# Mamba-2 scan of a hybrid decoder: one interruption of TensorE per group instead of four, cumulative sums spread by transfers

## Chip, cores and metric

The kernel runs on one core of a Trainium2 chip. The time is the device time of one execution of the whole program in microseconds; it was run three times before, and the median counts. Engines are called TensorE (PE), VectorE (DVE), ScalarE (ACT), GpSimd (POOL) and SyncE (SP).

## What is computed

Two layers over 256 tokens of width 2048, all in float32. A layer projects the normalised input by `w_in`, runs attention and a Mamba-2 mixer side by side, projects both by `w_out`, and adds a SwiGLU block. The part that matters here is the chunked scan, with 16 heads of 64 in 4 groups, a state of 128 and two chunks of 128 tokens:

```python
cum = cumsum(dt * a)                                   # within a chunk, per head
seg = cum_t[..., :, None] - cum_t[..., None, :]
decay = exp(where(causal, seg, -inf))                  # 128 x 128 for each head and chunk
cb = einsum('bclgn,bcsgn->bcgls', cc, bc)              # C times B, per group and chunk
y_diag = einsum('bcgkls,bcsgkp->bclgkp', cb[:, :, :, None] * decay, xdt)
states = einsum('bclgn,bclgk,bclgkp->bcgkpn', bc, decay_to_end, xdt)
y_off = einsum('bclgn,bcgkpn,bclgk->bclgkp', cc, prev, exp(cum))
```

The state of the first chunk is what the second starts from. `y_diag + y_off + d_skip * x` is gated and normalised later.

## The kernel before

**Pairs.** All big products go through one stream of pairs, 368 in a layer, 736 in all. A pair is two weight tiles of 128 x 512 f32 (512 KB in one transfer into `raw`, a ring of four). ScalarE rounds the pair to fp32r (`split`, L866), VectorE makes the remainder (`split_lo`, L1112), and TensorE forms high x high, low x high and high x low: 24 matmuls by 256 columns where weights are stationary (`products_turned`, L697, the first 32 pairs of a layer and the SwiGLU's first half), 12 matmuls by 512 columns elsewhere (`products`, L508). SyncE asks for a pair's tiles when the remainder of the pair four earlier is made.

**Order.** Every engine has its own loop over the layer's pairs `p`, and whatever else it does is written out by hand at a value of `p`. At `p`, ScalarE and VectorE split pair `p + 3` (`LEAD`), and ScalarE waits for TensorE to be done with pair `p - 1` first. So extras of ScalarE at `p` run from TensorE's start of pair `p` on, and those of VectorE a little later. TensorE does its extras of `p` behind the products of pair `p`. Each queue is in order: a wait stops all behind it on that engine.

**The scan.** Pairs 0 to 31 make the channels of the convolution (x, B, C). The step sizes are ready at pair 13; `cumulate` (p = 16) makes the cumulative sums by a matmul with a triangle of ones; `cum_out` (VectorE, p = 17, L1178) copies them to `cums`, negates them into `ncum` and cuts them into three bf16 parts (`cpart`). `turn_cum` (TensorE, p = 19, L593) turns the parts by two bf16 matmuls, and ScalarE copies them to `cumT` (p = 20). The scan goes in 8 units `u`, a group and a chunk each, over pairs 40 to 55:
- even `p`, `scan_a` (L602): four bf16 matmuls with a column of `pick` spread each head's sums over all partitions, one f32 matmul makes C times B. VectorE (`mask_cb`, L1236) adds `ncum` and the causal mask, ScalarE takes the exponential in halves (`decays`, L952), VectorE multiplies by C times B out of PSUM;
- odd `p`, `scan_b` (L620): four f32 matmuls by 64 columns (within the chunk) and one by 256 (the state of chunk 0, or its effect on chunk 1). ScalarE copies the state (L1060); VectorE's `y_out` (L1251) adds up. GpSimd's `scan_inputs` (L445) makes the factors `xdt`, `xde` and `dx`, at most two units ahead.

Around it, `evacuate` (ScalarE, L907) takes the projections q, k, v out of PSUM at p = 39, 47 and 55 with their squares, `qk_sum` (VectorE, L1225) adds the squares at p = 40, 48 and 56, `norm_qk` (GpSimd, L427) scales them, and `turn_qk` (TensorE, L637) turns them, behind pairs 45 and 51 (`KQ_TURNS`) and 59; `scale_qk` (ScalarE, L944) copies them out. From pair 56 on comes attention: `scores` (L649), softmax on VectorE and ScalarE, `turn_p`, `weigh_v` (L669), until pair 74.

Of the kernel before, what the change touches and what calls it, by code (L numbers as in the profile page):

```python
# [19 lines left out]
ALU = mybir.AluOpType  # L20
ACT = mybir.ActivationFunctionType
F32 = mybir.dt.float32
# [4 lines left out]
P = 128  # L27
# [13 lines left out]
def hybrid_decoder(nc, x, attn_norm_w, w_in, q_norm_w, k_norm_w, sinks, conv_w, conv_b, dt_bias, a_log,  # L41
# [40 lines left out]
    KQ_TURNS = [45, 51]  # L82
# [31 lines left out]
    with ctx:  # L114
# [32 lines left out]
        identb = sb("identb", [P, P], BF16)  # L147
        tri = sb("tri", [P, P])
        mask = sb("mask", [P, P])
# [30 lines left out]
        crest = sb("crest", [P, T, HS])  # L180
        PIECE = 32
        cpart = sb("cpart", [P, T, 4, PIECE], BF16)
        pick = sb("pick", [P, HS], BF16)
# [40 lines left out]
        decay = under("decay", [P, 2, HPG, P])  # L224
# [7 lines left out]
        cumT = nc.alloc_sbuf_tensor_at("cumT", [P, TOK], BF16, offset=placed["dtT"])  # L232
# [20 lines left out]
        cpart_ready, cumT_psum, cumT_ready = sem("cpart_ready"), sem("cumT_psum"), sem("cumT_ready")  # L253
# [6 lines left out]
        seg_psum, seg_masked, decay_ready, mt_ready = sem("seg_psum"), sem("seg_masked"), sem("decay_ready"), sem("mt_ready")  # L260
        xdt_ready, y_psum, state_ready, y_ready = sem("xdt_ready"), sem("y_psum"), sem("state_ready"), sem("y_ready")
# [100 lines left out]
        def _(pool):  # L362
# [8 lines left out]
            for s, credit in ((lo_split, RING), (pair_used, RING)):  # L371
# [9 lines left out]
            once(pool.tensor_copy(identb[:, :], ident[:, :]))  # L381
            once(pool.memset(mask[:, :], 0.0))
            once(pool.affine_select(out=mask[:, :], in_=mask[:, :], compare_op=ALU.is_ge, fill=NEG, base=0,
                                    pattern=[[1, P]], channel_multiplier=-1))
# [13 lines left out]
            once(pool.memset(cpart[:, :, :, :], 0.0))  # L398
            once(pool.tensor_tensor(crest[:, 0, :], ident[:, 0:HS], ident[:, PIECE:PIECE + HS], ALU.add))
            once(pool.tensor_tensor(pick[:, :], crest[:, 0, :], ident[:, 2 * PIECE:2 * PIECE + HS], ALU.add))  # L400
# [3 lines left out]
            for layer in range(DEPTH):  # L404
# [40 lines left out]
                def scan_inputs(u):  # L445

                    g, c = u // 2, u % 2
                    b = u % 2
# [8 lines left out]
                    if u == 0:  # L457
# [4 lines left out]
                    if u >= 2:  # L462
                        pool.wait_ge(y_ready, layer * 8 + (u - 1))
                    x_in = heads(ys[:, c, cols])
                    pool.tensor_tensor(heads(xdt[:, b, :]), x_in, spread(dt[:, c, hs]), ALU.mult).then_inc(xdt_ready, 1)
                    if c == 0:
                        pool.tensor_tensor(heads(xde[:, :]), x_in, spread(dte[:, hs]), ALU.mult).then_inc(xdt_ready, 1)
                    pool.tensor_tensor(heads(dx[:, b, :]), x_in, spread(dskip[:, hs]), ALU.mult).then_inc(xdt_ready, 1)

                def gate(z):  # L470
# [3 lines left out]
                    pool.wait_ge(y_ready, layer * 8 + 8)  # L474
# [9 lines left out]
                for u in (0, 1):  # L484
                    scan_inputs(u)
                norm_qk(0)
                for u in (2, 3, 4, 5):
                    scan_inputs(u)
                norm_qk(1)
                for u in (6, 7):  # L490
                    scan_inputs(u)
# [9 lines left out]
        def _(pe):  # L501
# [91 lines left out]
            def turn_cum(layer):  # L593

                pe.wait_ge(cpart_ready, layer + 1)
                for t in range(T):
                    last = nc.tensor.matmul(ps[:, 7, t * P:(t + 1) * P],
                                            cpart[:, t, :, :].rearrange("p a h -> p (a h)"), identb[:, :],
                                            start=True, stop=True)
                last.then_inc(cumT_psum, 1)  # L600

            def scan_a(layer, u):  # L602

                g, c = u // 2, u % 2
                if u == 0:
                    pe.wait_ge(silu_ready, layer * 4 + 4)
                    pe.wait_ge(cum_ready, layer + 1)
                    pe.wait_ge(cumT_ready, layer + 1)
                else:
                    pe.wait_ge(y_ready, layer * 8 + u)  # L610
                    pe.wait_ge(state_ready, layer * 4 + (u + 1) // 2)
                for k in range(HPG):
                    h = g * HPG + k
                    nc.tensor.matmul(ps[:, 6, k * P:(k + 1) * P], pick[:, h:h + 1].broadcast_to([P, P]),
                                     cumT[:, c * P:(c + 1) * P], start=True, stop=True)
                cols = slice(c * P, (c + 1) * P)
                nc.tensor.matmul(ps[:, 7, 0:P], bt[:, g, cols], ctm[:, g, cols], start=True, stop=True) \  # L617
                    .then_inc(seg_psum, 1)

            def scan_b(layer, u):  # L620

                g, c = u // 2, u % 2
                pe.wait_ge(mt_ready, layer * 8 + (u + 1))
# [821 lines left out]
```

## Time and profile before

| | us |
|---|---|
| runs | 2136.22, 2135.30, 2135.31 |
| median | 2135.31 |
| the profiled execution | 2136.34 |
| its span | 2134.6 |
| TensorE busy | 2127.5 |
| VectorE busy | 1235.5 |
| ScalarE busy | 990.9 |
| GpSimd busy | 114.2 |
| DMA, share of 16 engines busy | 61% |

The profile is one execution; its span runs from the first to the last instruction that the profiler saw. TensorE's granted clock is its full one, 2.4 GHz, in every slice of the span. TensorE's records overlap and their ends are modelled, so its pace is read from starts. An f32 matmul shows as two records, an fp32r product and a transpose as one.

### The profile page before, as it was taken

To read this page: it belongs to the slowest core of one execution; us is meant where nothing else is said; L and a number is where in the kernel's file an instruction comes from. 1 tells how busy PE (TensorE), PEld (TensorE's weight loads), DVE (VectorE), ACT (ScalarE), POOL (GpSimd) and SP (SyncE) were. 2 spreads that over 40 slices of the span, in tenths; PEclk is the share of its full clock that TensorE was granted. 3 is DMA by queue.
4 is the path that set the end of the run, shared out by engine and by line. 5 is a ranking of instruction groups with operands and counts; after the bars stand their busy time and mean duration, and the time that the engine had idled before them with its cause. 6 is when DMAs were issued, how large, how long until landed. Compare 5 with 4: busy or idle time off the path is not lost.

```text
span 2134.6 us, 34343 instructions
## 1 busy us (share of the span) xinstructions
PE 2127.5 (100%) x14793; PEld 1952.2 (91%) x14793; DVE 1235.5 (58%) x1464; ACT 990.9 (46%) x1269; POOL 114.2 (5%) x153
## 2 busy tenths in 40 slices
PE   9999999999999999999999999999999999999999
PEld 9988789999999999888899877899999999998887
DVE  5977865555555555544468778555555555554443
ACT  5555754444444444443445557544444444443332
POOL 2023200000000000000000222000000000000000
PEclk9999999999999999999999999999999999999999
DMA  7654456666666666555656544566666666666664
GB/s 221 181 170 133 130 188 189 192 194 196 191 196 193 193 198 192 189 192 193 190 160 188 158 137 132 191 183 196 191 197 194 193 197 191 195 195 201 205 198 138
DMA packets 203287, 392.76 MB, mean 184 GB/s; under 512 B 12240, under 2 KB 12608, under 8 KB 203136
## 3 DMA queue, kind: packets, MB, share of 16 engines
q1 hardware_dynamic: 202752, 390.24, 60.4%
q8 instruction: 116, 1.90, 0.3%
q0 software_dynamic: 352, 0.33, 0.2%
q14 instruction: 35, 0.29, 0.0%
q10 hardware_dynamic: 32, 0.01, 0.0%
HBM read 388.43 MB, written 2.10 MB: 183 GB/s over the span
## 4 chain that ended last, share of the span: by engine, by line
PE 98%; DVE 1%; ACT 1%; DMA 0%; issue 0%; ACTq 0%
PE ps L697 53%; PE ps L508 40%; PE ps L542 2%; PE ps L626 1%; PE ps L677 1%; PE ps L576 0%; PE ps L658 0%; PE ps L657 0%; DMA xr<-in_x_dram 0%; DVE w_lo L1112 0%; PE ps L617 0%; DVE sc L1271 0%; DVE mx L1275 0%; PE ps L533 0%; PE ps L634 0%; PE ps L631 0%
## 5 line engine op out<-in xcount | busy, mean ns | idle before, releaser
L697 PE MATMUL ps<-h_hi,w_hi_s 128*128 128x256 f32 x3320 | 920.7, 277 | 0.0
L697 PE MATMUL ps<-h_hi,w_lo_s 128*128 128x256 f32 x3320 | 918.7, 277 | 0.0
L697 PE MATMUL ps<-h_lo,w_hi_s 128*128 128x256 f32 x3320 | 918.7, 277 | 0.0
L1112 DVE TENSOR_TENSOR w_lo_s<-raw,w_hi_s 128x1024 fp32r<-128x1024 f32 x416 | 510.1, 1228 | 472.5 <-ACT w_hi_s L866 471.8
L866 ACT CAST w_hi_s<-raw 128x1024 fp32r<-128x1024 f32 x416 | 436.1, 1050 | 584.6 <-PE ps L697 559.6
L697 PEld LDWEIGHTS ps<-h_hi,w_hi_s 128*128 128x128 f32 x3320 | 624.7, 188 | 0.2
L697 PEld LDWEIGHTS ps<-h_lo,w_hi_s 128*128 128x128 f32 x3320 | 623.4, 188 | 0.1
L697 PEld LDWEIGHTS ps<-h_hi,w_lo_s 128*128 128x128 f32 x3320 | 623.4, 188 | 0.0
L1112 DVE TENSOR_TENSOR w_lo<-raw,w_hi 128x1024 fp32r<-128x1024 f32 x320 | 397.4, 1246 | 315.1 <-ACT w_hi L866 314.8
L866 ACT CAST w_hi<-raw 128x1024 fp32r<-128x1024 f32 x320 | 335.5, 1049 | 360.5 <-PE ps L508 340.7
L508 PE MATMUL ps<-w_hi,f_hi 128*128 128x512 f32 x956 | 296.3, 391 | 0.0
L508 PE MATMUL ps<-w_lo,f_hi 128*128 128x512 f32 x956 | 294.5, 389 | 0.0
L508 PE MATMUL ps<-w_hi,f_lo 128*128 128x512 f32 x956 | 294.4, 389 | 0.0
L508 PEld LDWEIGHTS ps<-w_lo,f_hi 128*128 128x128 f32 x956 | 179.4, 188 | 37.5
L508 PEld LDWEIGHTS ps<-w_hi,f_lo 128*128 128x128 f32 x956 | 179.4, 188 | 37.5
L508 PEld LDWEIGHTS ps<-w_hi,f_hi 128*128 128x128 f32 x956 | 177.8, 188 | 36.2 <-issue 0.3
L508 PE MATMUL ps<-w_hi,h_hi 128*128 128x512 f32 x320 | 106.1, 413 | 0.0
L508 PE MATMUL ps<-w_hi,h_lo 128*128 128x512 f32 x320 | 99.4, 392 | 0.0
L508 PE MATMUL ps<-w_lo,h_hi 128*128 128x512 f32 x320 | 99.0, 390 | 0.0
L508 PEld LDWEIGHTS ps<-w_hi,h_lo 128*128 128x128 f32 x320 | 60.0, 188 | 13.5
L508 PEld LDWEIGHTS ps<-w_lo,h_hi 128*128 128x128 f32 x320 | 60.1, 188 | 13.4
L508 PEld LDWEIGHTS ps<-w_hi,h_hi 128*128 128x128 f32 x320 | 56.4, 189 | 13.9 <-issue 4.6
(203 smaller groups left out, 989.4 us busy)
## 6 DMA issues: line engine op xcount, KB each, us to landing
raw<-in_w_gate_dram SPq DMA_DIRECT2D x176, 512.0 KB, 3.7
raw<-in_w_up_dram SPq DMA_DIRECT2D x176, 512.0 KB, 3.7
raw<-in_w_down_dram SPq DMA_DIRECT2D x176, 512.0 KB, 4.4
raw<-in_w_in_dram SPq DMA_DIRECT2D x144, 512.0 KB, 3.6
raw<-in_w_out_dram SPq DMA_DIRECT2D x64, 512.0 KB, 4.5
xr<-in_x_dram SPq DMA_DIRECT2D x4, 512.0 KB, 8.4
out_dram<-xr SPq DMA_DIRECT2D x3, 512.0 KB, 6.9
out_dram<-xr SPq DMA_DIRECT2D x2, 256.0 KB, 2.4
```

Source lines behind the costliest of these rows:

```text
L508: done = nc.tensor.matmul(ps[:, bank + t, :], lhs[:, rows + k, t * P:(t + 1) * P], w[:, slot, k, :], start=(first and k == 0 and w is w_hi ...
L542: done = nc.tensor.transpose(ps[0:src.shape[1], bank + at // N, at % N:at % N + src.shape[0]], src, ident[0:src.shape[0], 0:src.shape[0]])
L626: nc.tensor.matmul(ps[:, 7, 2 * P + k * HEAD:2 * P + (k + 1) * HEAD], decay[:, u % 2, k, :], xdt[:, u % 2, k * HEAD:(k + 1) * HEAD], start ...
L677: last = nc.tensor.matmul(ps[half * HEAD:(half + 1) * HEAD, 4, keys * P:TOK], vtok[:, keys, j, :], pT[:, half, keys * TOK:TOK + keys * P], ...
L697: done = nc.tensor.matmul(ps[:, bank + m // 2, m % 2 * TOK:(m % 2 + 1) * TOK], w[:, slot, k, m * P:(m + 1) * P], h[:, rows + k, :], start= ...
L866: nc.scalar.copy(split_buffers(p)[0][:, slot, :, :], raw[:, slot, :, :]).then_inc(hi_split, 1)
L1112: v_.tensor_tensor(lo[:, slot, :, :], raw[:, slot, :, :], hi[:, slot, :, :].bitcast(F32), ALU.subtract).then_inc(lo_split, 1)
```

## The change

`scan_a` and `scan_b` for 8 units go. In their place:
- `turn_cum` turns `cums` itself by two f32 transposes, and ScalarE copies 16 rows into `cum_rows` (p = 20). GpSimd (`spread_cum`) stores them in DRAM, waits, and reads each group's four rows back to all 128 partitions (`cum_all`), a transfer of 512 KB a group; each waits for the one before.
- `c_times_b` makes C times B of all groups and chunks behind pair 39, 8 matmuls in a row into two banks; `keep_cb` (VectorE, p = 40) copies it to SBUF times the triangle `tri`.
- `segments` (VectorE, p = 39, 43, 47, 51) makes the differences of a group, both chunks, by eight instructions, and cuts them at 0 from above; `decays` (ScalarE, p = 40, 44, 48, 52) takes one exponential of 128 x 1024; `times_cb` (VectorE, p = 41, 45, 49, 53) multiplies by C times B.
- `scan` (TensorE, behind pairs 42, 46, 50, 54) does a group's whole scan: the state of chunk 0, eight matmuls within the chunks, and, when ScalarE has copied the state, its effect on chunk 1. `y_out` follows at p = 43, 47, 51, 55.
- `turn_qk` 0 and 1 move from behind pairs 45 and 51 to behind 46 and 54, right after a scan.
- GpSimd's order becomes: spread 0, spread 1, factors of group 0, spread 2, `norm_qk(0)`, spread 3, factors of groups 1 and 2, `norm_qk(1)`, factors of group 3, `norm_qk(2)`. Factors of group g wait for `y_out` of group g - 1.
- `decay` is twice as large; `decay`, `cb` and `cum_all` lie where the mixer's outputs go later. `mask`, `identb`, `cpart`, `crest` and `pick` and what builds them are gone. The buffers of the products stay where they are.

Of the diff, the lines that are taken out stand in the functions above and are left out here, but for the first; new semaphores too.

```diff
@@ -79,7 +79,8 @@
...
     CONV_TURNS = [15, 22, 30]
-    KQ_TURNS = [45, 51]
+    KQ_TURNS = [46, 54]
+    SCAN = [42, 46, 50, 54]
     def weights_stationary(p):
@@ -229,7 +223,13 @@
...
+        cum_rows = nc.alloc_sbuf_tensor_at("cum_rows", [HS, TOK], F32, offset=placed["dtT"])
+        cum_kept = nc.dram_tensor("cum_kept", [DEPTH, HS, TOK], F32, kind="Internal").ap()
+
+
+        cum_all = nc.alloc_sbuf_tensor_at("cum_all", [P, HS, TOK], F32, offset=at_hi)
+        cb = nc.alloc_sbuf_tensor_at("cb", [P, T, GROUPS, P], F32, offset=at_lo)
+        decay = nc.alloc_sbuf_tensor_at("decay", [P, 2, T, HPG, P], F32, offset=at_lo + T * GROUPS * P * 4)
@@ -442,10 +438,20 @@
...
+                def spread_cum(g):
+
+                    hs = slice(g * HPG, (g + 1) * HPG)
+                    if g == 0:
+                        pool.wait_ge(cum_rows_ready, layer + 1)
+                        pool.dma_start(cum_kept[layer, :, :], cum_rows[:, :]).then_inc(cum_stored, 16)
+                        pool.wait_ge(cum_stored, 16 * (layer + 1))
+                    else:
+                        pool.wait_ge(cum_landed[g - 1], 16 * (layer + 1))
+                    pool.dma_start(cum_all[:, hs, :], cum_kept[layer, hs, :].partition_broadcast(P)) \
+                        .then_inc(cum_landed[g], 16)
+
+                def scan_inputs(g):
+
@@ -454,24 +460,25 @@
...
+                    if g == 0:
...
+                    else:
+                        pool.wait_ge(y_ready, layer * 4 + g)
+                    for c in range(T):
+                        x_in = heads(ys[:, c, cols])
+                        if c == 0:
+                            pool.tensor_tensor(heads(xde[:, :]), x_in, spread(dte[:, hs]), ALU.mult).then_inc(xdt_ready, 1)
+                        pool.tensor_tensor(heads(xdt[:, c, :]), x_in, spread(dt[:, c, hs]), ALU.mult).then_inc(xdt_ready, 1)
+                        pool.tensor_tensor(heads(dx[:, c, :]), x_in, spread(dskip[:, hs]), ALU.mult).then_inc(xdt_ready, 1)
...
+                    pool.wait_ge(y_ready, layer * 4 + GROUPS)
@@ -481,14 +488,16 @@
...
+                spread_cum(0)
+                spread_cum(1)
+                scan_inputs(0)
+                spread_cum(2)
...
+                spread_cum(3)
+                scan_inputs(1)
+                scan_inputs(2)
...
+                scan_inputs(3)
@@ -592,47 +601,40 @@
...
+                pe.wait_ge(cum_ready, layer + 1)
+                turned(7, [(t * P, cums[:, t, :]) for t in range(T)], rows_psum)
+
+            def c_times_b(layer):
+
+                pe.wait_ge(silu_ready, layer * 4 + 4)
+                pe.wait_ge(cum_rows_ready, layer + 1)
+                for c in range(T):
+                    cols = slice(c * P, (c + 1) * P)
+                    for g in range(GROUPS):
+                        last = nc.tensor.matmul(ps[:, 6 + c, g * P:(g + 1) * P], bt[:, g, cols], ctm[:, g, cols],
+                                                start=True, stop=True)
+                last.then_inc(cb_psum, 1)
+
+            def scan(layer, g):
+
+                def within(c):
+                    for k in range(HPG):
+                        nc.tensor.matmul(ps[:, 6, c * GW + k * HEAD:c * GW + (k + 1) * HEAD], decay[:, g % 2, c, k, :],
+                                         xdt[:, c, k * HEAD:(k + 1) * HEAD], start=True, stop=True)
+
+                if g == 0:
+                    pe.wait_ge(tok_ready, layer * 3 + 3)
+                    pe.wait_ge(cb_ready, layer + 1)
...
+                    pe.wait_ge(y_ready, layer * 4 + g)
+                pe.wait_ge(xdt_ready, layer * 20 + 5 * (g + 1))
+                pe.wait_ge(mt_ready, layer * 4 + (g + 1))
+                nc.tensor.matmul(ps[:, 7, 0:GW], btok[:, g, :], xde[:, :], start=True, stop=True).then_inc(state_psum, 1)
+                for c in range(T):
+                    within(c)
+                pe.wait_ge(state_ready, layer * 4 + (g + 1))
+                nc.tensor.matmul(ps[:, 7, GW:2 * GW], ctm[:, g, P:2 * P], state[:, :], start=True, stop=True) \
+                    .then_inc(y_psum, 1)
@@ -767,8 +769,10 @@
...
+                        if p == 39:
+                            c_times_b(layer)
+                        if p in SCAN:
+                            scan(layer, SCAN.index(p))
@@ -949,11 +953,10 @@
...
+            def decays(layer, g):
+                act.wait_ge(seg_ready, layer * 4 + (g + 1))
+                d = decay[:, g % 2, :, :, :]
+                nc.scalar.activation(d, d, ACT.Exp).then_inc(decay_ready, 1)
@@ -1041,8 +1044,8 @@
...
+                        act.wait_ge(rows_psum, layer + 1)
+                        nc.scalar.copy(cum_rows[:, :], ps[0:HS, 7, 0:TOK]).then_inc(cum_rows_ready, 1)
@@ -1051,13 +1054,11 @@
...
+                    if p + 2 in SCAN:
+                        decays(layer, SCAN.index(p + 2))
+                    if p in SCAN:
+                        act.wait_ge(state_psum, layer * 4 + (SCAN.index(p) + 1))
+                        nc.scalar.copy(state[:, :], ps[:, 7, 0:GW]).then_inc(state_ready, 1)
@@ -1233,34 +1228,42 @@
...
+            def keep_cb(layer):
+
+                dve.wait_ge(cb_psum, layer + 1)
+                for c in range(T):
+                    ins = v_.tensor_tensor(cb[:, c, :, :], ps[:, 6 + c, :].rearrange("p (g l) -> p g l", g=GROUPS),
+                                           tri[:, :].unsqueeze(1).broadcast_to([P, GROUPS, P]), ALU.mult)
+                ins.then_inc(cb_ready, 1)
+                dve.wait_ge(cb_ready, layer + 1)
+
+            def segments(layer, g):
+
+                dve.wait_ge(cum_landed[g], 16 * (layer + 1))
+                for c in range(T):
+                    for k in range(HPG):
+                        h = g * HPG + k
+                        ins = v_.tensor_scalar(decay[:, g % 2, c, k, :], cum_all[:, h, c * P:(c + 1) * P],
+                                               ncum[:, c, h:h + 1], 0.0, ALU.add, ALU.min)
+                ins.then_inc(seg_ready, 1)
+
+            def times_cb(layer, g):
+                dve.wait_ge(decay_ready, layer * 4 + (g + 1))
+                for c in range(T):
+                    d = decay[:, g % 2, c, :, :]
+                    ins = v_.tensor_tensor(d, d, cb[:, c, g, :].unsqueeze(1).broadcast_to([P, HPG, P]), ALU.mult)
...
+            def y_out(layer, g):
+
+                dve.wait_ge(y_psum, layer * 4 + (g + 1))
+                y, d = ys[:, :, g * GW:(g + 1) * GW], dx[:, 1, :]
+                v_.tensor_tensor(y[:, 0, :], ps[:, 6, 0:GW], dx[:, 0, :], ALU.add)
+                own.done(v_.tensor_tensor(d, ps[:, 6, GW:2 * GW], d, ALU.add))
+                own.done(v_.tensor_tensor(
+                    y[:, 1, :].rearrange("p (h d) -> p h d", d=HEAD), ps[:, 7, GW:2 * GW].rearrange("p (h d) -> p h d", d=HEAD),
+                    ecum[:, g * HPG:(g + 1) * HPG].unsqueeze(2).broadcast_to([P, HPG, HEAD]), ALU.mult))
+                v_.tensor_tensor(y[:, 1, :], y[:, 1, :], d, ALU.add).then_inc(y_ready, 1)
@@ -1386,8 +1387,14 @@
...
+                    if p - 1 in SCAN:
+                        y_out(layer, SCAN.index(p - 1))
+                    if p + 3 in SCAN:
+                        segments(layer, SCAN.index(p + 3))
+                    if p == 40:
+                        keep_cb(layer)
+                    if p + 1 in SCAN:
+                        times_cb(layer, SCAN.index(p + 1))
```

## Rows read from the trace of the kernel before

**Rows 1.** The page: busy time of TensorE, and the chain that ended last
```profile
PE 2127.5 (100%) x14793; PEld 1952.2 (91%) x14793; DVE 1235.5 (58%) x1464; ACT 990.9 (46%) x1269; POOL 114.2 (5%) x153
...
PE 98%; DVE 1%; ACT 1%; DMA 0%; issue 0%; ACTq 0%
```

**Rows 2.** Waits of TensorE, the whole run: us in total, times, longest us
```profile
PE ps L721 <- POOL numbers L377: 2.2, 1, 2.2
...
PE ps L677 <- DVE pT L1284: 0.3, 2, 0.2
```

**Rows 3.** Timeline of TensorE, layer 0: start us, us, engine, line, operation, tiles, count
```profile
128.72 0.62 PE L508 MATMUL ps<-w_hi,h_lo 128*128 128x512 f32 x2
...
133.25 0.61 PE L508 MATMUL ps<-w_lo,h_hi 128*128 128x512 f32 x2
...
141.18 0.40 PE L614 MATMUL ps<-cumT,pick 128*128 128x128 bf16 x4
141.42 0.44 PE L617 MATMUL ps<-ctm,bt 128*128 128x128 f32 x2
141.61 0.71 PE L508 MATMUL ps<-w_hi,h_hi 128*128 128x512 f32 x2
...
144.47 1.00 PE L626 MATMUL ps<-xdt,decay 128*128 128x64 f32 x8
145.30 0.65 PE L634 MATMUL ps<-state,ctm 128*128 128x256 f32 x2
145.60 0.82 PE L508 MATMUL ps<-w_hi,h_hi 128*128 128x512 f32 x2
...
148.56 0.40 PE L614 MATMUL ps<-cumT,pick 128*128 128x128 bf16 x4
```

**Rows 4.** Timeline of TensorE: first spread of the scan and first scores, both layers
```profile
133.71 0.40 PE L614 MATMUL ps<-cumT,pick 128*128 128x128 bf16 x4
...
194.66 0.50 PE L657 MATMUL ps<-kT,qT 64*128 64x128 f32 x4
...
1194.93 0.40 PE L614 MATMUL ps<-cumT,pick 128*128 128x128 bf16 x4
...
1255.89 0.50 PE L657 MATMUL ps<-kT,qT 64*128 64x128 f32 x4
```

**Rows 5.** Timeline of TensorE around the first `turn_qk`, layer 0
```profile
151.85 1.00 PE L626 MATMUL ps<-xdt,decay 128*128 128x64 f32 x8
...
153.17 1.04 PE L542 MATMUL ps<-ident,acc 128*128 128x128 f32 x8
...
156.80 0.40 PE L614 MATMUL ps<-cumT,pick 128*128 128x128 bf16 x4
```

**Rows 6.** Timeline of VectorE, layer 0: a split, masking, `y_out`, square sums
```profile
156.48 1.23 DVE L1112 TENSOR_TENSOR w_lo<-raw,w_hi 128x1024 fp32r<-128x1024 f32 x1 [2.68 <-ACT w_hi L866]
157.62 1.12 DVE L1241 SCALAR_TENSOR_TENSOR decay<-ps,ncum,mask 128x128 f32<-128x128 f32 x4
...
161.61 0.42 DVE L1259 TENSOR_TENSOR dx<-ps,dx 128x256 f32<-128x256 f32 x1 [0.21 <-PE ps L634]
...
162.53 0.42 DVE L1263 TENSOR_TENSOR ys<-ys,dx 128x256 f32<-128x256 f32 x1
...
167.16 1.28 DVE L1232 TENSOR_REDUCE ssq<-ps 128x8 f32<-128x512 f32 x2
```

**Rows 7.** Groups of VectorE by shape: busy us, mean ns of one
```profile
L1215 DVE TENSOR_SCALAR acc<-stage,vecs 128x256 f32<-128x256 f32 x32 | 13.0, 408 | 0.1
```

**Rows 8.** Timeline of VectorE and GpSimd, layer 0: a split beside a product of GpSimd
```profile
147.58 1.63 DVE L1112 TENSOR_TENSOR w_lo<-raw,w_hi 128x1024 fp32r<-128x1024 f32 x1
...
148.09 1.59 POOL L465 TENSOR_TENSOR xdt<-ys,dt 128x256 f32<-128x256 f32 x1
```

**Rows 9.** The page: landing of weight tiles; and the waits of ScalarE on them
```profile
raw<-in_w_in_dram SPq DMA_DIRECT2D x144, 512.0 KB, 3.6
...
ACT w_hi_s L866 <- DMA raw<-in_w_in_dram: 1.3, 2, 1.1
```

More of the change, by code:

```diff
@@ L252, in hybrid_decoder @@
         dtT_ready, dt_turned = sem("dtT_ready"), sem("dt_turned")
-        cpart_ready, cumT_psum, cumT_ready = sem("cpart_ready"), sem("cumT_psum"), sem("cumT_ready")
+        rows_psum, cum_rows_ready = sem("rows_psum"), sem("cum_rows_ready")
+        cum_stored, cum_landed = sem("cum_stored"), [sem(f"cum_landed{g}") for g in range(4)]
         dt_abs, dt_exp, dta_ready = sem("dt_abs"), sem("dt_exp"), sem("dta_ready")
@@ L593, in turn_cum @@
             def turn_cum(layer):
[L595 to L608, printed above, removed]
-                else:
[L610 to L618, printed above, removed]
@@ L620, in scan_b @@
-            def scan_b(layer, u):
-                g, c = u // 2, u % 2
-                pe.wait_ge(mt_ready, layer * 8 + (u + 1))
-                pe.wait_ge(xdt_ready, layer * 20 + (5 * g + 3 + 2 * c))
-                for k in range(HPG):
-                    nc.tensor.matmul(ps[:, 7, 2 * P + k * HEAD:2 * P + (k + 1) * HEAD], decay[:, u % 2, k, :],
-                                     xdt[:, u % 2, k * HEAD:(k + 1) * HEAD], start=True, stop=True)
-                if c == 0:
-                    if g == 0:
-                        pe.wait_ge(tok_ready, layer * 3 + 3)
-                    last = nc.tensor.matmul(ps[:, 6, 0:GW], btok[:, g, :], xde[:, :], start=True, stop=True)
-                else:
-                    pe.wait_ge(state_ready, layer * 4 + (g + 1))
-                    last = nc.tensor.matmul(ps[:, 6, 0:GW], ctm[:, g, P:2 * P], state[:, :], start=True, stop=True)
-                last.then_inc(y_psum, 1)
+                pe.wait_ge(cum_ready, layer + 1)
@@ L651, in scores @@
                 if a == 0:
-                    pe.wait_ge(y_ready, layer * 8 + 8)
+                    pe.wait_ge(y_ready, layer * 4 + GROUPS)
                 else:
@@ L769, in _ @@
                             conv_out(layer, CONV_TURNS.index(p))
-                        if 40 <= p < 56:
-                            (scan_a, scan_b)[p % 2](layer, (p - 40) // 2)
+                        if p == 39:
+                            c_times_b(layer)
+                        if p in SCAN:
+                            scan(layer, SCAN.index(p))
                         if p in KQ_TURNS:
@@ L950, in scale_qk @@
                 last.then_inc(qkT_ready, 1)
-            def decays(layer, u):
-                for half in range(2):
-                    act.wait_ge(seg_masked, layer * 16 + (2 * u + half + 1))
-                    d = decay[:, u % 2, 2 * half:2 * half + 2, :]
-                    nc.scalar.activation(d, d, ACT.Exp).then_inc(decay_ready, 1)
+            def decays(layer, g):
+                act.wait_ge(seg_ready, layer * 4 + (g + 1))
+                d = decay[:, g % 2, :, :, :]
+                nc.scalar.activation(d, d, ACT.Exp).then_inc(decay_ready, 1)
             def exps(layer, a):
@@ L1043, in _ @@
                     if p == 20:
-                        act.wait_ge(cumT_psum, layer + 1)
-                        nc.scalar.copy(cumT[:, :], ps[:, 7, 0:TOK]).then_inc(cumT_ready, 1)
+                        act.wait_ge(rows_psum, layer + 1)
+                        nc.scalar.copy(cum_rows[:, :], ps[0:HS, 7, 0:TOK]).then_inc(cum_rows_ready, 1)
                     if p == 19:
@@ L1053, in _ @@
                         to_tokens(layer, CONV_TURNS.index(p))
-                    if 40 <= p < 56:
-                        u = (p - 40) // 2
-                        if p % 2 == 0:
-                            decays(layer, u)
-                        elif u % 2 == 0:
-                            act.wait_ge(y_psum, layer * 8 + (u + 1))
-                            nc.scalar.copy(state[:, :], ps[:, 6, 0:GW]).then_inc(state_ready, 1)
+                    if p + 2 in SCAN:
[3 more added lines that the diff above has]
+                        nc.scalar.copy(state[:, :], ps[:, 7, 0:GW]).then_inc(state_ready, 1)
                     if p in KQ_TURNS:
@@ L1388, in _ @@
                         cum_out(layer)
-                    if 40 < p < 56:
-                        (mask_cb, y_out)[p % 2](layer, (p - 40) // 2)
+                    if p - 1 in SCAN:
[6 more added lines that the diff above has]
+                        times_cb(layer, SCAN.index(p + 1))
                     if p in (40, 48, 56):
```

72 lines of the change are left out of this document (4 added, 68 removed).

## Prediction

> **What bounds the kernel now.** I read the page first: TensorE is busy for 2127.5 us of the span of 2134.6, and the chain that ended last runs over TensorE for 98% of it [rows 1]. Then I asked what TensorE waited for: its longest wait in the whole run is 2.2 us at the start, and all its waits on other engines come to some 3 us [rows 2]. So the time is the length of TensorE's own instruction stream, and a change pays by what it takes out of that stream and costs what it makes TensorE wait. The span is 1.7 us short of its execution's 2136.34 us, and that is 1.03 us above the median of 2135.31; I take differences within the execution and set them on the median. About 0.2% (4.3 us) is what a measurement here can tell from no change.
>
> **The price of an interruption.** I read TensorE's timeline by starts, because the ends overlap. Undisturbed, 20 products take from 128.72 to 133.25, so a pair of 12 takes 2.72 us [rows 3]. `scan_a` and the next pair take from 141.18 to 144.47, 3.29 us, so this interruption costs 0.57. Of it the four bf16 spreads (`pick`) take 0.24, C times B 0.19 to the next start; 0.21 is what its two passes are worth at the pace below, and about 0.12 is left, which shows as slower first products behind it. `scan_b` and its pair take from 144.47 to 148.56, 4.09 us, so 1.37: the four matmuls by 64 columns run as 8 records in 0.83 (0.104 each), the one by 256 columns is worth twice two passes, 0.43, and again some 0.12 is left [rows 3]. I call 0.12 the price of breaking the products. Each f32 matmul is two records, and a pass by 64 columns costs the same 0.10 as one by 128, so the weight load sets it.
>
> **The stretch before.** From the first insertion behind pair 40 to the first scores behind pair 56 it is 194.66 - 133.71 = 60.95 us in layer 0, and 1255.89 - 1194.93 = 60.96 in layer 1 [rows 4]. Sixteen pairs are 43.49; 17.46 us is the scan with two `turn_qk` (4.95 against 4.09 us for the interval with it, 0.86 each [rows 5]).
>
> **The stretch after, if TensorE never waits.** One C times B block: 8 matmuls, 16 passes at 0.104 = 1.66, with the break 1.78. Four scans, each 0.43 (state) + 16 passes at 0.104 = 1.66 (within) + 0.43 (off) + 0.12 = 2.64: 10.56. Two `turn_qk`, still glued to a scan: 1.72. Sum 14.06, against 17.46: 3.40 less. As a check from the other side: 32 bf16 spreads at 0.06 are 1.92 and 11 breaks fewer (16 to 5) at 0.12 are 1.32, 3.24 in all; the rest is what the first unit lost. `turn_cum` exchanges two bf16 matmuls at 0.06 for two f32 transposes at 0.10 (8 in about 0.8 [rows 5]): +0.1. So -3.3 us in a layer, -6.6 in both.
>
> **What may become late.** I walk the in-order queues of ScalarE and VectorE against TensorE. An f32 product of two tensors by 1024 columns repeats every 1.14 us [rows 6] and needs 1.22 alone, so VectorE makes about one column in 1.04 ns, and an instruction behind another costs about 0.07 more. `segments` is eight tensor_scalars by 128 columns; the trace has none of this shape. The nearest row is the same operation, SBUF to SBUF with pointer scalars, 408 ns at 256 columns [rows 7]: 0.27 alone at 128 and about 0.20 in a row, 1.6 for eight. The upper bound is the old masking, four in 1.12 [rows 6], 0.28 each, 2.2 for eight; the lower bound is two columns at a time, 0.13 each, 1.0 for eight. I take 1.6. `times_cb` and `keep_cb` are two by 512 columns, as the reduce that takes 1.28 [rows 6]: 1.25. `y_out` for both chunks is two gaps of 0.46 and two of 0.34 [rows 6]: 1.60.
> The tightest place is the scan of group 2 behind pair 50, since evacuation, square sums, `turn_qk` 0 and group 2's factors meet there. Count from TensorE's end of pair 46. Scan 1 lasts to 2.52; `turn_qk` and the break to 3.50; pair 50 ends at 3.50 + 4 x 2.72 = 14.37. VectorE's split of pair 50 starts 3.31 behind the start of `turn_qk`, as now from 153.17 to 156.48 [rows 5, 6], at 5.83. From there it has no gap: split 1.14, `y_out` 1.60, `segments` 1.60 (10.17), split of 51, 1.14 + 0.4 because GpSimd's `scan_inputs(2)` runs then (a split beside GpSimd took 1.63 and GpSimd 1.59 [rows 8]) (11.71), square sums 1.20, split of 52, 1.14, `times_cb` 1.25: 15.30, and TensorE sees it at 15.36. It waits 1.0 us. At the two bounds of `segments`, with and without the crowding, this is 0.0 to 1.6, and to 2.4 if two more instructions are crowded. The same walk leaves 0.6 us of slack at group 0 (Exp's table is loaded first, C times B's product stands ahead), 1.7 at groups 1 and 3, and 0.3 at the first scores, where `y_out` of group 3 comes late and two pairs without a break between make TensorE sooner; I put 0.1 there. Where a split is late it has 4 us or more before its pair is used. The state copy takes 0.6 us with its hand-over and hides under 1.66 us of within-chunk matmuls. What GpSimd does for a group waits only for the previous `y_out` and is ready 3 us before its scan, `norm_qk` and the last broadcast ahead of it included; this cover would go if the group's five products took 6 us instead of 3 to 4.
> The transfers: per layer one store of 16 KB and four broadcasts of 512 KB, each as large as a weight tile, which lands in 3.6 us [rows 9]. Three are issued between pairs 21 and 30 and the last near pair 43, each needed 10 us or more later. A weight tile is asked for when the split four pairs earlier ends and is cast at the start of its fourth pair ahead: 5 us of slack behind its 3.6, and 5 more before TensorE needs it. ScalarE's largest visible wait on weight tiles is 1.3 us in all [rows 9]. I cost them at nothing. The constants dropped at the start (mask, bf16 identity, picks) were built by GpSimd under the first pairs: nothing. The buffers of the products keep their places, so their pace stays.
> **Sum:** -3.3 + 1.0 + 0.1 = -2.2 us in a layer, -4.4 in all: 2131.9 against the profiled 2136.34, or 2130.9 against the median.
>
> **A rule of the skill against the row.** The row says that VectorE's tensor_scalar on f32 makes one column at a time (408 ns for 256; at two it would need about 0.28). The Trainium skill, VectorE: DVE Perf Modes, section "Mode 2×_2P — use both read ports for one tensor", says that an f32 tensor_scalar between SBUF operands gets two. By that rule `segments` would be as its lower bound; by the row it is 1.6, and I go by the row.
>
> **Rivals.**
> - No wait worth the name. `segments` at its lower bound ends 0.6 us sooner and without crowding another 0.4: the wait is about 0, and the whole 6.6 us arrive less 0.2: 2128.9. This is the outcome that the skill's rule above gives. Against it speak the tensor_scalar row and the crowded split. Chance 0.22.
> - VectorE becomes the bound in the stretch: `segments` at 0.28 each, three crowded instructions, and the delay carries into the scores. Each layer waits 2.0 to 3.0 us: 2132.7 to 2134.7, 2133.5 as its middle. For it: VectorE has 9 us of work without a gap there. Chance 0.17.
> - A break has no price of its own: the 0.12 belongs to the f32 passes themselves. Then only the spreads go, 1.92 + 0.2 - 0.1 = 2.0 in a layer, less the wait of 1.1: -1.8 in all, 2133.5. Against it: slow first products behind each of the 16 insertions. Chance 0.04.
> - Slower: the broadcasts hold up weight tiles between pairs 21 and 33. All eight read a few rows for 128 partitions, and no row shows such a transfer. It decides from the point where one of them delays a tile by over 10 us. If each takes three times a weight tile, 10.8 us, and blocks the tiles behind it, TensorE loses 0.8 at each, 6.4 in all: 2130.9 + 6.4 = 2137.3. The Trainium skill, DMA: Bandwidth & Descriptors, section "SWDGE vs HWDGE vs iDMA", says that an engine takes turns between the queues of GpSimd and of the others, which speaks against blocking; no row here shows both kinds at once under load. Chance 0.07.
>
> **How the numbers follow.** The forecast has 0.50. A wait under 1.06 us a layer puts it past 0.2% (2131.0), a larger one leaves it within: 0.27 and 0.23. Faster: 0.27 + 0.22 = 0.49. Same: 0.23 + 0.17 + 0.04 = 0.44. Slower 0.07. The range takes in no wait with 0.35 us more saved in a layer, 2128.0, and waits of 3 us a layer, 2134.8.
>
> **What would show it.** Between the first insertion behind pair 39 and the first scores, TensorE's timeline should take 17 x 2.72 + 14.06 = 60.3 us and about 1.1 of waits; scans at 2.64 each; a wait of TensorE on VectorE's product with C times B of about 1 us, once a layer, at the third scan; `segments` at 0.27 us alone; broadcasts of 4 to 6 us that nobody waits for. The forecast is wrong if TensorE waits elsewhere, above all in the products or at the scores, if the third scan does not wait, or if breaks saved do not shorten the stream.

## The result, and the profile after

The changed kernel takes 2142.53 us (median of six, 2142.34 to 2145.16) against 2135.49 for the one before beside it: a ratio of 1.0035, with a 95% interval of 1.0025 to 1.0044. It is slower, by 7.0 us, where 4.4 us less were forecast, and it lies outside the range of 2128.0 to 2134.8 us. The profiled execution took 2142.81 us, 6.5 more than the profiled one before.

The page of the changed kernel, as [rows 1], and its waits of TensorE (us in total, times, longest), as [rows 2]:

```profile
PE 2126.7 (99%) x14729; PEld 1954.1 (91%) x14729; DVE 1236.8 (58%) x1444; ACT 988.0 (46%) x1245; POOL 118.9 (6%) x157
...
PE 96%; DVE 2%; ACT 1%; issue 1%; DMA 0%; ACTq 0%
```

```profile
PE ps L632 <- DVE decay L1254: 4.9, 2, 2.4
PE ps L551 <- DVE mx L1283: 2.6, 2, 1.3
...
```

Two waits are new, each once a layer: the scan of group 2 waits 2.4 us for the product with C times B, and the third `turn_qk`, behind pair 59, waits 1.3 us for VectorE's second score. In the kernel before, the timelines of TensorE and of VectorE have this `turn_qk` and the end of the score it needs as

```profile
205.65 1.07 PE L542 MATMUL ps<-ident,stage 128*128 128x128 f32 x8
```

```profile
205.35 0.15 DVE L1280 TENSOR_TENSOR mx<-sink,mx 128x4 f32<-128x4 f32 x1
```

The score ended at 205.50, so the margin was 0.15 us.

ScalarE's evacuation of q, which stands at the head of the work that leads to this score, starts at the end of pair 55, here in the kernel before and in the changed one:

```profile
190.67 1.27 ACT L918 ACTIVATE stage<-ps,rs 128x512 f32<-128x512 f32 x2 [0.26 <-PE ps L508]
```

```profile
193.27 1.27 ACT L922 ACTIVATE stage<-ps,rs 128x512 f32<-128x512 f32 x2 [0.56 <-PE ps L517]
```

The first scores start at 194.66 [rows 4] and at 195.88 (below), so the evacuation was 3.99 us ahead of them and is now 2.61 ahead: behind pair 55 no `scan_b` stands any more that held TensorE back. Of these 1.38 us the margin covers 0.15, and 1.23 are left of the 1.28 that were measured.

TensorE's timeline, layer 0, with the extras of the scan (start us, us, engine, line, tiles, count; as [rows 3, 4]):

```profile
130.95 1.95 PE L614 MATMUL ps<-ctm,bt 128*128 128x128 f32 x16
...
140.91 0.59 PE L632 MATMUL ps<-xde,btok 128*128 128x256 f32 x2
141.34 1.89 PE L622 MATMUL ps<-xdt,decay 128*128 128x64 f32 x16
143.07 0.65 PE L636 MATMUL ps<-state,ctm 128*128 128x256 f32 x2
...
171.52 0.67 PE L632 MATMUL ps<-xde,btok 128*128 128x256 f32 x2 [2.43 <-DVE decay L1254]
...
195.88 0.50 PE L659 MATMUL ps<-kT,qT 64*128 64x128 f32 x4
```

From C times B to the first scores it is 195.88 - 130.95 = 64.93 us, and 66.56 in layer 1. In the kernel before the same stretch, from the end of pair 39, took 60.95 + 2.72 = 63.67 [rows 4, 3]. Both layers make the same moves, yet the second is 1.6 us longer. TensorE's timeline behind the wait in layer 1, and a table of stretches (columns: us, busy us and count of PE, PEld, DVE, ACT and POOL, granted clock, DMA share, GB/s), show why:

```profile
1235.10 1.02 PE L632 MATMUL ps<-xde,btok 128*128 128x256 f32 x2 [2.44 <-DVE decay L1254]
1235.91 3.52 PE L622 MATMUL ps<-xdt,decay 128*128 128x64 f32 x16
1239.22 1.17 PE L636 MATMUL ps<-state,ctm 128*128 128x256 f32 x2
```

```profile
160.00:170.00 10.00, 9.09 (x41) 7.18 (x39) 9.49 (x17) 6.71 (x9) 3.78 (x6) 1.00 0.27 75
170.00:174.00 4.00, 2.48 (x19) 2.46 (x20) 2.93 (x5) 1.32 (x2) 3.84 (x3) 0.97 0.78 216
174.00:178.00 4.00, 4.00 (x12) 3.16 (x12) 3.77 (x6) 0.00 (x0) 3.92 (x3) 0.61 0.78 252
...
1234.00:1236.00 2.00, 0.90 (x3) 0.76 (x4) 2.00 (x3) 0.00 (x0) 2.00 (x1) 0.82 0.65 179
1236.00:1242.00 6.00, 6.00 (x24) 5.43 (x23) 2.82 (x6) 1.31 (x2) 5.34 (x5) 0.50 0.75 227
1242.00:1244.00 2.00, 2.00 (x10) 1.67 (x9) 2.00 (x6) 0.00 (x0) 1.82 (x4) 0.97 0.00 0
```

Behind the wait of layer 1 the granted clock is 0.50, which is 1.2 GHz instead of 2.4, and the sixteen passes take 3.52 us instead of 1.89. In layer 0 the clock stays full for some 2 us more and falls for a shorter time. By the clock column, 4 x 0.03 + 4 x 0.39 = 1.7 us are lost in layer 0 and 2 x 0.18 + 6 x 0.50 + 2 x 0.03 = 3.4 in layer 1. The third `turn_qk`'s wait of 1.28 us has no such thing behind it.

Now VectorE and GpSimd before the wait, layer 0; the first line is `segments` for group 0, for comparison:

```profile
130.71 1.65 DVE L1246 TENSOR_SCALAR decay<-cum_all,ncum 128x128 f32<-128x128 f32 x8
...
162.82 0.42 DVE L1266 TENSOR_TENSOR ys<-ys,dx 128x256 f32<-128x256 f32 x1
163.17 3.54 DVE L1246 TENSOR_SCALAR decay<-cum_all,ncum 128x128 f32<-128x128 f32 x8
166.62 1.22 DVE L1113 TENSOR_TENSOR w_lo<-raw,w_hi 128x1024 fp32r<-128x1024 f32 x1
167.76 1.28 DVE L1227 TENSOR_REDUCE ssq<-ps 128x8 f32<-128x512 f32 x2
168.96 1.22 DVE L1113 TENSOR_TENSOR w_lo<-raw,w_hi 128x1024 fp32r<-128x1024 f32 x1
170.09 1.29 DVE L1254 TENSOR_TENSOR decay<-decay,cb 128x512 f32<-128x512 f32 x2
```

```profile
163.33 0.61 POOL L473 TENSOR_TENSOR xde<-ys,dte 128x256 f32<-128x256 f32 x1 [14.64 <-DVE ys L1266]
163.90 0.61 POOL L474 TENSOR_TENSOR xdt<-ys,dt 128x256 f32<-128x256 f32 x1
...
165.62 0.61 POOL L475 TENSOR_TENSOR dx<-ys,dskip 128x256 f32<-128x256 f32 x1
```

The end of `y_out` releases both `segments` (by VectorE's queue) and GpSimd's factors (by its semaphore), so they run side by side. The eight instructions, 1.65 us for group 0 where GpSimd is still, take 3.54. GpSimd's five products keep their step of 0.57 us.

### The profile page after: what moved, and what is told of

Same layout as the page of the kernel before. It is cut to its first block, busy times and chain, and to the rows that moved or that the text cites. A ratio compares the mean times of both kernels' runs of the same rounds, so it can differ in the third digit from the quotient of the medians.

```text
span 2141.1 us, 34156 instructions
## 1 busy us (share of the span) xinstructions
PE 2126.7 (99%) x14729; PEld 1954.1 (91%) x14729; DVE 1236.8 (58%) x1444; ACT 988.0 (46%) x1245; POOL 118.9 (6%) x157
## 4 chain that ended last, share of the span: by engine, by line
PE 96%; DVE 2%; ACT 1%; issue 1%; DMA 0%; ACTq 0%
PE ps L699 53%; PE ps L517 38%; PE ps L551 2%; PE ps L622 1%; DVE w_lo L1113 1%; PE ps L679 1%; DVE mx L1278 0%; DVE sc L1274 0%; PE ps L585 0%; DVE decay L1246 0%; ACT sc L966 0%; ACT w_hi L870 0%; DVE ssq L1227 0%; PE ps L636 0%; DMA xr<-in_x_dram 0%
```

## Experiments

Each stands beside runs of the kernel before on its chip, whose median was 2135.4 to 2135.9 us. In each case theory and rival are as on record before the run.

**1. Fill the wait.** Ten idle products of ident with itself go to TensorE ahead of the wait at scan 2; nothing else changes.

```diff
+                if g == 2:
+                    pe.wait_ge(qkT_ready, layer * 3 + 1)
+                    for _ in range(10):
+                        nc.tensor.matmul(ps[:, 5, 0:P], ident[:, :], ident[:, :], start=True, stop=True)
```

> TensorE makes ten idle f32 matmuls (about 2.1 us) where it waited 2.43 us for group 2's factors in each layer. Theory (the wait makes the clock fall, and the fall costs 5.2 us in both layers): the wait shrinks to 0.2 to 0.4 us, the granted clock stays 1.00 everywhere, about 2137.3 us, 5 less than the changed kernel. Rival (the clock falls because of the long run of f32 passes, whatever came before): the fall stays, 2142.5 or more.

Measured: 2139.58 us (2137.59 to 2140.65), ratio 1.0017 [1.0007, 1.0026], the profiled execution 2137.59, with the mean clock at 1.000 in all ten. The scan still starts as late as before (0.2 us of its wait are left), the fill only takes the place of the wait, and 5.2 us of the profiled time are gone. By the clock column the fall had cost 5.1 us, so the two agree, and the waits alone do not explain the result. But 5.2 is one execution, the fastest of ten. By the medians the gain is only 3.0 us: six of the ten times lie 2 to 3 us above the profiled one, with the clock at full, and what they hold stays open. The rival, a fall that comes whatever stood ahead of the passes, is out.

**2. GpSimd's factors behind the segments.** The factors of groups 1 to 3 wait for `seg_ready` too.

```diff
                         pool.wait_ge(y_ready, layer * 4 + g)
+                        pool.wait_ge(seg_ready, layer * 4 + g + 1)
```

> GpSimd starts the factors of groups 1 to 3 only when the group's segments are made. Theory (the segments took 3.54 us instead of 1.65 because GpSimd's five products ran beside them): segments 1.65 us in every group, wait before scan 2 about 0.9 us instead of 2.43, no fall of the clock, 2134 to 2135. Rival (segments are slow for another reason, as the place or the landing of the spread sums): 3.5 us again, 2142.5.

Measured: 2136.85 us (2135.38 to 2140.87), ratio 1.0009 [0.9999, 1.0019]. The durations of the eight segments of group 2 (ns, least, median, most) and the timeline of VectorE behind them:

```profile
L1247 DVE TENSOR_SCALAR decay<-cum_all,ncum x8: 277/279/280, 162.9 to 164.3; 128x128 f32<-128x128 f32 x8
```

```profile
166.81 1.58 DVE L1114 TENSOR_TENSOR w_lo<-raw,w_hi 128x1024 fp32r<-128x1024 f32 x1
168.31 2.12 DVE L1255 TENSOR_TENSOR decay<-decay,cb 128x512 f32<-128x512 f32 x2
```

In the changed kernel the same eight were 276/649/660. So what slowed them was GpSimd, and nothing in themselves; the rival is out. But the wait went only from 2.4 to 1.8 us, not to the expected 0.9: the factors now run beside a split (1.58 instead of 1.22) and the product with C times B (2.12 instead of 1.29), 1.2 us of the 1.9 won. Crowding was moved more than removed. In eight of ten executions the mean clock stayed full, in two it was lower (2140.87 and 2140.78 us). Only the profiled execution, one of the eight, has a trace; if the wait was 1.8 us in the two as well, a wait of this length lowers the clock sometimes.

**3. Segments one pair earlier.** They then run where GpSimd has nothing to do for group 2.

```diff
-                    if p + 3 in SCAN:
-                        segments(layer, SCAN.index(p + 3))
+                    if p + 4 in SCAN:
+                        segments(layer, SCAN.index(p + 4))
```

> Segments are made one pair earlier, out of the rush behind pair 47 and away from GpSimd's factors. Theory: segments 1.65 us, wait before scan 2 at most 0.3 us, clock 1.00, and the waits of 1.28 us before the last turn_qk stay: 2142.5 - 10 = 2132 to 2133. If even this waits over 1 us there, the evacuation and the square sums set it. Rival (merging gains nothing on TensorE, breaks have no price): 2136 to 2138 without any wait at scan 2.

Measured: 2133.84 us (2132.81 to 2134.79), ratio 0.9993 [0.9984, 1.0002], clock full in all ten. The waits of TensorE:

```profile
PE ps L551 <- DVE mx L1283: 2.6, 2, 1.3
PE ps L723 <- POOL numbers L380: 2.2, 1, 2.2
PE ps L632 <- DVE decay L1254: 1.2, 2, 0.6
```

`segments` for group 2 takes 1.64 us. The wait at scan 2 is 0.6 us, where at most 0.3 were expected. This one step, moved by a pair, takes 8.7 us off the changed kernel: 3.7 of wait and the whole fall of the clock. The `turn_qk` wait is untouched, so it is a matter of its own.

**4. Each broadcast twice.** The second lands in a buffer that nobody reads; the chain of transfers still goes one after the other.

```diff
+                    pool.dma_start(cum_again[:, :, :], cum_kept[layer, hs, :].partition_broadcast(P)) \
+                        .then_inc(cum_extra, 16)
```

> Every broadcast of cumulative sums is made twice, the second copy into a place that nobody reads: 4.2 MB more. Theory (the transfers are hidden): within 0.5 us of the changed kernel, 2142.0 to 2143.0. Rival (the broadcasts hold up weight tiles): up by 2 us or more, with ScalarE waiting for raw in the pairs 21 to 45. GpSimd issues a little more ahead of group 1's factors, 0.6 us, which has 3 us of slack.

Measured: 2143.06 us (2138.07 to 2145.4), ratio 1.0033 [1.002, 1.0046]; against the changed kernel's 2142.5 no difference that can be told. The transfers are not the cause. In its fastest execution, the profiled one, the 2.5 us wait of layer 0 left the clock at full; behind the one of layer 1 it fell.

**5 and 6. The price of a break.** The kernel before, with 320 idle f32 products in the SwiGLU: one behind each of 320 pairs, or four behind each fourth.

```diff
+                        if c and q % 4 == 3:
+                            for _ in range(4):
+                                nc.tensor.matmul(ps[:, 5, 0:P], ident[:, :], ident[:, :], start=True, stop=True)
```

> The kernel before, with one idle product of two fp32 passes put behind each of the 320 pairs of the SwiGLU's chunks 1 to 10 (both layers). Its passes cost the same as in the kernel with four behind every fourth pair: 640 passes at 0.104 us from rows 3's kind, 66.6 us. Theory (each interruption of the pairs costs 0.12 us, whatever stands in it): 320 breaks, 66.6 + 38.4 us over the kernel before, about 2240.5 us, and 28.8 us more than the kernel with 80 breaks. Rival (a break has no price and the 6.7 us that TensorE's stream got shorter came from elsewhere, from the products that went): the same time as that kernel, about 2202 us.

> The kernel before, with four idle products of two fp32 passes behind every fourth pair of the SwiGLU's chunks 1 to 10: the same 320 products as in the kernel with one behind each pair, in 80 breaks instead of 320. Theory (0.12 us for each break): 66.6 + 9.6 us over the kernel before, about 2211.7 us, 28.8 us less than that kernel. Rival (no price): the same time as that kernel.

Measured: 2227.04 and 2207.79 us, ratios 1.0428 [1.0409, 1.0447] and 1.0338 [1.0319, 1.0357]. The same work in 240 breaks more costs 19.25 us, 0.080 a break; the rest, 2207.79 - 2135.86 - 80 x 0.080 = 65.5 us, is 0.102 for each of 640 passes. A break has a price of its own, so the rival is out, but it is two thirds of the 0.12 expected, and both kernels are faster than expected. The price was measured between products of 256 columns, while the scan stands between products of 512.

**7. Waits alone, elsewhere.** The kernel before, with 20 waits of 2.5 us in the SwiGLU, where there is no scan.

```diff
+                        if c and q == 2:
+                            pe.wait_ge(lo_split, base + (P_FF + c * PER_FF + q) + 3 + (1 + RING))
```

> The kernel before, with TensorE made to wait at the third pair of the gate in chunks 1 to 10 of the SwiGLU (20 places, some 43 us apart) until VectorE has split the weights three pairs further on, which starts when the pair before is done: a wait of 0.25 + 1.05 + 1.22 us, about 2.5 us, as long as the one at scan 2. Theory (the fall of the granted clock to 0.5 behind scan 2's wait is the wait's doing): the clock falls behind most of these 20 waits, each fall costing the 1.7 to 3.5 us seen behind scan 2, so 2135.5 + 50 + 34 to 70 = 2219 to 2255 us and a mean clock of 0.98. Rival (the fall needs more than the wait: the scan's kind of work beside it): the clock stays at 1.0 and the time is 2135.5 + 50 = about 2185 us.

Measured: 2220.79 us (2219.88 to 2221.69), ratio 1.0399 [1.038, 1.0418], mean clock 0.988. TensorE's waits, one of them in its timeline, and the stretches behind it:

```profile
PE ps L697 <- DVE w_lo_s L1114: 49.0, 20, 2.5
```

```profile
691.00 0.58 PE L697 MATMUL ps<-h_hi,w_hi_s 128*128 128x256 f32 x1 [2.45 <-DVE w_lo_s L1114]
...
693.94 0.41 PE L697 MATMUL ps<-h_lo,w_hi_s 128*128 128x256 f32 x1
694.15 0.41 PE L697 MATMUL ps<-h_hi,w_lo_s 128*128 128x256 f32 x1
...
695.79 0.28 PE L697 MATMUL ps<-h_hi,w_hi_s 128*128 128x256 f32 x1
695.90 0.28 PE L697 MATMUL ps<-h_lo,w_hi_s 128*128 128x256 f32 x1
```

```profile
690.00:692.00 2.00, 1.00 (x4) 1.00 (x5) 0.94 (x1) 0.00 (x0) 0.00 (x0) 0.75 0.63 239
692.00:694.00 2.00, 2.00 (x12) 2.00 (x11) 0.00 (x0) 0.00 (x0) 0.00 (x0) 0.50 0.85 255
694.00:696.00 2.00, 2.00 (x17) 2.00 (x17) 0.00 (x0) 0.30 (x1) 0.00 (x0) 0.89 0.02 6
```

Products of 256 columns start 0.21 us apart at 1.2 GHz and 0.11 at 2.4. In stretches of 5 us over the whole span the clock is low behind 15 of the 20 waits, 25.6 us lost in all, 1.7 for each fall. So a wait of 2.45 us is enough without the scan, and whether a given wait does it is not certain. Of the 84.9 us over the kernel before, 49.0 are waits and 25.6 the clock; the other 10.3, 0.5 at each place, are not traced.

**8. Two more steps of VectorE's order.** On experiment 3: the product with C times B for group 2 at pair 48 ahead of the square sums, and the first score ahead of pair 59's split and of the third square sums.

```diff
+                    if p == 56:
+                        score(layer, 0)
                     if base + p + LEAD < ALL:
                         split_lo(base + p + LEAD)
...
-                    if p + 1 in SCAN:
+                    if p == 48:
+                        times_cb(layer, 2)
+                    if p in (41, 45, 53):
                         times_cb(layer, SCAN.index(p + 1))
```

> The kernel with the segments one pair earlier (2133.84 us), and two more steps of VectorE's order: group 2's product with C times B stands ahead of the sums of the second query chunk's squares (at pair 48 instead of 49), and the first score's work ahead of pair 59's split and the third sum of squares. Theory (the two waits left, 0.60 us at scan 2 and 1.28 us at the third turning of queries in each layer, are VectorE's order alone): both go under 0.2 us, 2133.8 - 2 x (0.6 + 1.28) = 2130.1 us, within 1 us of the forecast of 2130.9 us. Rival (the wait moves on: a split comes late for its pair, or the third chunk's scaling on GpSimd is late since the sum of squares now is): a new wait of over 0.8 us a layer, 2132 us or more.

Measured: 2137.15 us (2136.4 to 2137.89), ratio 1.0006 [0.9997, 1.0015]: the theory held for scan 2 and fell for the third `turn_qk`, where the rival came true. Its longest wait of TensorE, and GpSimd's work that it waited for:

```profile
PE ps L551 <- POOL stage L438: 5.4, 2, 2.7
```

```profile
197.57 1.13 POOL L415 TENSOR_TENSOR rqv<-ssq,numbers 128x16 f32<-128x16 f32 x1 [15.21 <-DVE ssq L1227]
...
199.07 3.08 POOL L417 TENSOR_TENSOR rq<-rqv,numbers 128x16 f32<-128x16 f32 x1
202.23 3.11 POOL L438 TENSOR_TENSOR stage<-stage,rq 128x512 f32<-128x512 f32 x2
```

The wait at scan 2 is gone. The square sums, now last, feed a chain of GpSimd that takes 7.8 us here (5.6 in experiment 3). The order had served the score at the expense of a longer chain. Behind the wait of 2.68 us the clock stayed full in layer 0 and fell in layer 1, for 1.7 us.

**9. Square sums first.** The same, but the third square sums stand ahead of the first score.

```diff
                     if p == 56:
+                        qk_sum(layer, 2)
                         score(layer, 0)
```

> The reordered kernel with one step put right: the third sum of squares stands ahead of the first score's work, and that ahead of pair 59's split (in the kernel before this one the sum stood behind both, and TensorE waited 2.7 us in each layer for GpSimd's scaling of the third chunk). By that trace's durations the sum ends at 193.6 us, GpSimd's three power steps 3.5 us later and its scaling at 199.2 to 200.2; VectorE's second score ends near 202.2; TensorE ends pair 59 and the turning behind it at 202.7. Theory (both waits are the order's alone): neither scan 2 nor the third turning waits over 0.3 us, the clock stays at 1.0, and the time is 2137.15 - 2 x 2.7 - 1.7 (the fall of the clock in layer 1) = about 2130 us. Rival (GpSimd and VectorE slow each other, as GpSimd's 3.11 us instead of 2.05 showed, wherever they meet): a wait of 0.5 to 1.5 us a layer is left, 2131 to 2133 us.

Measured: 2130.13 us (2129.47 to 2131.08), ratio 0.9976 [0.9966, 0.9985], clock full in all ten: faster than both kernels. TensorE's waits, and its timeline from C times B to the third `turn_qk`:

```profile
PE ps L723 <- POOL numbers L380: 2.2, 1, 2.2
PE ps L551 <- DMA xr<-in_x_dram: 0.8, 1, 0.8
PE ps L679 <- DVE pT L1287: 0.3, 2, 0.2
```

```profile
130.88 1.95 PE L614 MATMUL ps<-ctm,bt 128*128 128x128 f32 x16
...
191.54 0.50 PE L659 MATMUL ps<-kT,qT 64*128 64x128 f32 x4
...
201.80 0.82 PE L551 MATMUL ps<-ident,sc 128*128 128x128 f32 x6
202.73 1.06 PE L551 MATMUL ps<-ident,stage 128*128 128x128 f32 x8
```

Nothing of the scan waits. The stretch takes 191.54 - 130.88 = 60.66 us in both layers, 3.0 less than before.

**10. The changed kernel again.**

> The changed kernel itself, again, beside the others on this chip, to see in how many executions the clock falls behind the wait at scan 2. Theory (the fall comes behind most but not all waits of 2.4 us, and where it comes it costs 1.7 to 3.5 us): times between 2137.5 (no fall: 2142.8 - 5.2) and 2145, the mean clock below 1.0 in all those above 2139. Rival (the fall comes every time): all within 0.5 us of 2142.5.

Measured: 2142.42 us, ratio 1.0031 [1.0019, 1.0044]; the five times are 2140.13, 2142.37, 2142.42, 2142.62 and 2142.65, the first with a mean clock of 0.999, the others with 0.997 or 0.998. The size of the fall differs between executions, as the theory had it, but none of the five was free of it, and four of them lie within 0.5 us of 2142.5, as the rival had it. The profiled one (2142.42) waits 2.44 us at scan 2 in both layers, and its clock is full behind the first and falls behind the second, for 3.4 us. So not every such wait lowers it. It also waits 0.82 us at scan 3 in layer 0, as the profiled execution of experiment 1 does (0.83); the profiled changed kernel of the result does not.

## Why the prediction was wrong

Three terms of the sum failed. `segments` was taken at its length alone, and beside GpSimd it took more than twice that, so the wait at scan 2 was 2.43 us instead of 1.0. The wait of the third `turn_qk`, 1.28 us a layer, was not in the sum. And a wait was priced at its own length, while the clock fell behind it.

**What bounds the kernel** held: each change of the time is a change of TensorE's stream, of its waits, or of its clock.

**The stream, -3.3 us a layer,** was right to 0.4. Experiment 9, where nothing of the scan waits, shows 60.66 us against 60.3 forecast for the stretch, and 2130.17 against the profiled 2136.34 before: -6.2 for the forecast's -6.6. In its trace the two scans without a `turn_qk` behind them, those of groups 0 and 2, cost 2.70 and 2.72 us instead of 2.64; that makes up some 0.2 to 0.3 of the missing 0.4. That a break costs 0.08 rather than 0.12 where it was measured alone does not explain it, since the breaks of the kernel before are part of its measured 17.46 us.

**`segments`, 1.6 us,** was right for an undisturbed one (1.65) and wrong where it mattered. The walk gave the split of pair 51 the crowding with `scan_inputs(2)`. But the factors are released by the same `y_out` that VectorE has just finished, so they meet what stands next in VectorE's queue, and that is `segments`. It took 3.54. Put into the walk in place of 1.6, with the split back at 1.14: 15.36 + 1.94 - 0.4 = 16.90, against pair 50's end at 14.37, a wait of 2.5; 2.43 was measured. This is the term that put the wait past the forecast and close to the VectorE rival's 2 to 3 us.

**The wait at the scores, 0.1 us,** looked at the wrong place. The scores did not wait, but the third `turn_qk` behind pair 59 also waits for the second score, and that was never walked. It stood 0.15 us clear before; the two pairs without a break ahead of the scores made TensorE come 1.38 us sooner against ScalarE's evacuation, and the chain from there over square sums and scores did not get shorter. Cost: 1.28 us a layer. With an order of VectorE that suits it, it is gone (experiment 9).

**The clock was not priced at all.** The forecast took each wait at its length. By the clock column the falls behind the two waits at scan 2 cost 5.1 us, as much as the waits themselves (4.9). This term follows from the first: with `segments` at 1.6 the wait would have been about 1.0 us, and behind the waits of 0.6 and 1.3 us in experiment 3 the clock stayed full in all ten executions. But with the two waits as they were, it makes most of the loss: without it the sum below is +1.3 us. None of the rivals held it: the VectorE rival came close in mechanism, with 2133.5 us, but without the clock.

**The other rivals.** The lower bound of 1.0 us for `segments`, two columns at a time, did not come, with or without GpSimd beside it, and with it the rival without a wait fell. A break has a price (experiments 5 and 6). The change did come out slower, but not by the path of the slower rival.

**The sum again,** in the profiled executions: -6.2 for the stream (experiment 9), +4.9 for scan 2, +2.6 for `turn_qk`, +5.1 for the clock: +6.4, and 2142.81 - 2136.34 = +6.5 was measured.

**The transfers,** costed at nothing, cost nothing. The row of the changed kernel's DMA issues (KB each, median us from issue to landing), as [rows 9]:

```profile
cum_all<-cum_kept POOLq DMA_DIRECT2D x8, 512.0 KB, 5.6
```

They land in 4.8 to 6.7 us, where 4 to 6 were forecast, and doubled they change nothing that can be told (experiment 4), so the slower rival is out.

## What to carry to other kernels

Where one instruction releases work on GpSimd and the next in VectorE's own queue, cost that next one as if crowded, or move it: here one step moved by a pair was worth 8.7 us of 2142.

Shortening TensorE's stream uses up the slack of every wait behind it. List all its semaphore waits in the stretch with their margins before, also the ones that cost nothing; a margin of 0.15 us was one of the two losses here.

A wait of TensorE as long as 2.4 us is to be priced with what may follow it at 1.2 GHz, here mostly another 1.7 to 3.4 us and sometimes nothing; waits of 0.6 and 1.3 us cost their own length alone.

## What the runs showed of the hardware

- VectorE's f32 tensor_scalar from SBUF to SBUF, 128 columns, lasts 0.28 us, and in a row one starts every 0.20, as the row for 256 columns made one expect [rows 7]: 128 columns more cost 408 - 280 = 128 ns, one column in 1.0 ns. Beside GpSimd's products of two SBUF tensors its median is 649 ns, about the length of one such product (0.61), while these keep their step of 0.57 us. The Trainium skill, SBUF — State Buffer, section "Who interferes with whom", says that a VectorE instruction with at most one SBUF input contends with GpSimd only in its two-port modes, and that there the engine that issues first keeps the shared ports for its whole instruction and blocks the other. The 649 ns would fit such blocking, which no row shows directly. The pace is about that of VectorE's products of two tensors (1024 columns in 1.14 us [rows 6]) and speaks against a two-port mode, so the condition does not seem to fit this case.
- With two SBUF inputs on VectorE both sides lost: the product with C times B took 2.12 us instead of 1.29, a split 1.58 instead of 1.22 (experiment 2), and GpSimd's scaling 3.11 instead of 2.05 (experiments 8 and 3).
- TensorE's granted clock fell to 1.2 GHz behind 15 of 20 waits of 2.45 us (experiment 7), behind one of two of 2.68 us (experiment 8), in 2 of 10 executions of experiment 2, whose profiled one waits 1.8 us, and in none of the ten of experiment 3, whose profiled one waits 0.6 and 1.3 us.
